# Gate and up projections as 2x2 block products with seven block products each, from the seventh pair of tiles on

## The chip, the cores and the metric

The kernel runs on one core of a Trainium2 chip. The metric is the device time of one execution in microseconds (us). The core has a matrix engine (PE, with its weight loads shown apart as PEld), a vector engine (DVE), a scalar engine (ACT), GpSimd (POOL) and a sync engine (SP), which here issues DMAs. Each engine runs its own instructions in order; they wait for each other through semaphores.

## The reference, cut to what matters

Two transformer blocks run over 512 tokens of width 1024, all in float32. The second block has two feed-forward layers (SwiGLU) of width 2816, and the change is in the first two matrix products of each.

```
D_FF = 2816
def swiglu(x, w_gate, w_up, w_down):
    return (jax.nn.silu(x @ w_gate) * (x @ w_up)) @ w_down

def second_block(x, ...):
    h = x
    f = swiglu(rms_norm(h, g_ffn1_pre[i]), w_ffn1_gate[i], w_ffn1_up[i], w_ffn1_down[i])
    h = h + 0.5 * rms_norm(f, g_ffn1_post[i])
    ...                      # attention
    f = swiglu(rms_norm(h, g_ffn2_pre[i]), w_ffn2_gate[i], w_ffn2_up[i], w_ffn2_down[i])
    h = h + 0.5 * rms_norm(f, g_ffn2_post[i])
    ...
```

## The kernel before

All activations lie transposed, features on the 128 partitions and the 512 tokens along the row. A float32 product is made of three matmuls on the fp32r type (`mm3`, lines 283 to 287): each operand is split into a high part, which ScalarE makes by a copy to fp32r, and a low part, which VectorE makes by subtracting the high part. The three are high by high, low activation by high weight, and high activation by low weight.

The weights are one stream of 218 chunks of 128 rows by 1024 (512 KB). A chunk holds the eight 128x128 tiles, one for each block of 128 input features, that make one tile of 128 output features. SP loads chunk d into slot d % 4 of `RAW`; ScalarE writes its high part to `WH` (`hi_of_weights`, line 622 in the profile, where all of ScalarE's operations are counted), VectorE overwrites `RAW` with its low part (`WL`; `lo_of_weights`, line 1110, and line 1462 in the loop). Counting semaphores order it: `w_hi`, `w_lo` and `mm` count chunks whose high part, low part and matmuls are done; SP loads chunk d when chunk d - 4 has been multiplied.

A feed-forward layer starts with `mlp_up` (chunks D_F1 = 40 to 83, and D_F2 = 140 to 183 of the second layer): 22 pairs of tiles, where a pair is a gate chunk and the up chunk of the same 128 hidden features. The first four chunks run in halves of 256 tokens, since their input is still being normalised; the other 40 are a hardware loop (`Fori(1, 11)`) of ten rounds over four PSUM banks, each chunk 8 x 3 matmuls of 512 columns. `UH` and `UL` hold the input without the factor 1/rms of each token, so VectorE multiplies each product by it (`T[6]`) when it empties the bank: lines 1466 for gate and 1468 for up. ScalarE takes the Silu, VectorE multiplies the two (line 1471), ScalarE writes the high part of the result to `HH` and VectorE the low part to `HL` (line 1473). `f_g`, `f_s`, `f_u`, `f_h`, `f_hh` and `f_hl` count these steps. GpSimd has nothing to do in `mlp_up`; around it, it adds squares for the norms (`sum_y`, `sum_n`, lines 514 and 525).

`mlp_down` follows without a break: 16 chunks at 512 columns and then a tail at 256 columns (`TAIL_H`, `TAIL_L`). `plan_banks` says which event frees each bank; `DOWN_BANK` lists the banks of `mlp_down`.

## Time and profile before

| what | value |
|---|---|
| median of 3 runs | 1502.83 us (1502.73 to 1506.14) |
| the profiled execution, first to last instruction | 1500.5 us |
| PE busy | 1452.3 us (97%) |
| VectorE, ScalarE, GpSimd busy | 828.7, 683.7, 201.9 us |
| chain that ended last | PE 84%, DVE 9%, ACT 3% |
| the 40 full chunks of `mlp_up`, first layer | 217.6 us, from 428.2 to 645.8 us |

The page of the profile gives the totals. Its chain is the path from the last instruction back to what released each one, so it tells which engine sets the end. A matmul's duration in the profile runs over the start of the next one, so the pace of a row of matmuls is read from the distance of their starts. Times "from the start" are from the first instruction of the profiled execution.

### The profile page before, as it was taken

Reading aid. Unit: us, or ns where it says so; the run is one execution under the profiler, and the core shown is the slowest. Engines: PE = TensorE matmul, PEld = TensorE weight load, DVE = VectorE, ACT = ScalarE, POOL = GpSimd, SP = SyncE. Lnnn points to the kernel's source line nnn. Section 1 sums busy time; section 2 is a strip of 40 time slices with the busy share of each in tenths; the row PEclk is TensorE's granted clock in tenths of the full one; section 3 lists DMA queues with packets and bytes.
Section 4 is the critical chain, followed back from the end, with each engine's and each line's share of the span. In section 5 each row is a group of like instructions: output and inputs, shape, how many; then the busy total and the mean of one; then the engine's idle time right before and its main releaser. Section 6 shows DMA issues by size and latency. Waiting matters only on the chain.

```text
span 1500.5 us, 22048 instructions
## 1 busy us (share of the span) xinstructions
PE 1452.3 (97%) x8524; PEld 1226.9 (82%) x8524; DVE 828.7 (55%) x1455; ACT 683.7 (46%) x1302; POOL 201.9 (13%) x319
## 2 busy tenths in 40 slices
PE   7999999899999999999999999989999999999997
PEld 4887876678988888888998777769988888888996
DVE  6678646776645444432275577574754444422474
ACT  4565536676542222221363556676532232321563
POOL 0000000443310000000130222451300000000221
PEclk9999999999999999999999999999999999999999
DMA  9542440004033333333404211503133333332321
GB/s 365 197 167 85 124 157 10 1 2 169 2 99 98 98 98 98 94 95 94 152 3 167 71 57 43 169 16 99 33 109 98 94 92 96 103 105 92 120 85 56
DMA packets 42148, 146.71 MB, mean 98 GB/s; under 512 B 4673, under 2 KB 7121, under 8 KB 41682
## 3 DMA queue, kind: packets, MB, share of 16 engines
q1 hardware_dynamic: 37986, 128.99, 27.2%
q0 software_dynamic: 3072, 15.71, 2.8%
q8 instruction: 54, 0.88, 0.3%
q10 hardware_dynamic: 1008, 0.89, 0.2%
q14 instruction: 28, 0.23, 0.0%
HBM read 141.39 MB, written 4.19 MB: 97 GB/s over the span
## 4 chain that ended last, share of the span: by engine, by line
PE 84%; DVE 9%; ACT 3%; issue 2%; DMA 1%; POOL 0%; DVEq 0%; SPq 0%; ACTq 0%; POOLq 0%
PE B L285 22%; PE B L287 22%; PE B L286 22%; PE CROW_P L285 3%; PE CROW_P L287 3%; PE CROW_P L286 3%; PE B L1789 2%; PE B L2025 1%; DVE AL L1381 1%; DVE WADA L1143 1%; PE CROW_P L1868 1%; ACT T L622 1%; PE CROW_P L1768 1%; ACT AH L622 1%; DVE WL L1110 1%
## 5 line engine op out<-in xcount | busy, mean ns | idle before, releaser
L285 PE MATMUL B<-UH,WH 128*128 128x512 f32 (+1 forms) x1008 | 374.7, 372 | 4.6 <-DVE WL L1110 3.7
L287 PE MATMUL B<-UH,WL 128*128 128x512 f32 (+1 forms) x1008 | 372.3, 369 | 0.0
L286 PE MATMUL B<-UL,WH 128*128 128x512 f32 (+1 forms) x1008 | 372.3, 369 | 0.0
L622 ACT ACTIVATE WH<-RAW 128x1024 fp32r<-128x1024 f32 x174 | 182.6, 1052 | 120.0 <-DMA RAW<-in_stream 111.6
L285 PEld LDWEIGHTS B<-UH,WH 128*128 128x128 f32 x1008 | 190.4, 189 | 38.0 <-issue 5.0
L286 PEld LDWEIGHTS B<-UL,WH 128*128 128x128 f32 x1008 | 190.3, 189 | 32.0
L287 PEld LDWEIGHTS B<-UH,WL 128*128 128x128 f32 x1008 | 190.2, 189 | 32.0
L1110 DVE TENSOR_TENSOR WL<-RAW,WH 128x1024 fp32r<-128x1024 f32 x94 | 116.0, 1240 | 143.8 <-ACT WH L622 143.7
L1462 DVE TENSOR_TENSOR WL<-RAW,WH 128x1024 fp32r<-128x1024 f32 x80 | 98.0, 1226 | 76.7 <-ACT WH L622 73.9
L622 ACT ACTIVATE T<-B 128x256 f32<-128x256 f32 (+5 forms) x186 | 86.5, 465 | 109.9 <-PE B L287 63.3
L622 ACT ACTIVATE T<-T 128x512 f32<-128x512 f32 (+3 forms) x131 | 68.7, 525 | 130.8 <-DVE T L1466 119.2
L514 POOL TENSOR_TENSOR T<-T,T 128x256 f32<-128x256 f32 x60 | 55.0, 918 | 543.0 <-ACT T L622 542.2
L622 ACT ACTIVATE HH<-T 128x512 f32 (+1 forms) x44 | 27.8, 632 | 189.3 <-DVE T L1471 183.3
L285 PE MATMUL B<-HH,WH 128*128 128x512 f32 x192 | 74.7, 389 | 0.0
L286 PE MATMUL B<-HL,WH 128*128 128x512 f32 x192 | 74.7, 389 | 0.0
L287 PE MATMUL B<-HH,WL 128*128 128x512 f32 x192 | 74.7, 389 | 0.0
L285 PE MATMUL B<-UH,KEPT_H 128*128 128x256 f32 (+1 forms) x220 | 66.4, 302 | 1.6 <-DVE KEPT_L L1108 1.6
L1468 DVE TENSOR_TENSOR T<-B,T 128x512 f32<-128x512 f32 x40 | 27.7, 692 | 71.2 <-PE B L287 71.2
L286 PE MATMUL B<-UL,KEPT_H 128*128 128x256 f32 (+1 forms) x220 | 65.9, 299 | 0.0
L287 PE MATMUL B<-UH,KEPT_L 128*128 128x256 f32 (+1 forms) x220 | 65.7, 299 | 0.0
L1381 DVE TENSOR_TENSOR AL<-CROW_P,AH 128x128 fp32r<-128x128 f32 (+3 forms) x96 | 42.5, 483 | 17.3 <-ACT AH L622 17.1
L1473 DVE TENSOR_TENSOR HL<-T,HH 128x512 f32 x40 | 27.7, 693 | 36.6 <-ACT HH L622 36.6
(419 smaller groups left out, 3146.2 us busy)
## 6 DMA issues: line engine op xcount, KB each, us to landing
RAW<-in_stream SPq DMA_DIRECT2D x202, 512.0 KB, 3.7
WADA<-in_w_ada SPq DMA_DIRECT2D x8, 1024.0 KB, 16.7
RAW<-in_stream SPq DMA_DIRECT2D x16, 384.0 KB, 3.5
WADA<-in_w_ada SPq DMA_DIRECT2D x2, 2048.0 KB, 11.5
W<-in_w POOLq DMA_DIRECT2D x2, 2048.0 KB, 12.1
X<-in_x SPq DMA_DIRECT2D x2, 1024.0 KB, 11.0
DECAY<-in_decay POOLq DMA_DIRECT2D x1, 2048.0 KB, 9.6
X<-in_x POOLq DMA_DIRECT2D x2, 1024.0 KB, 8.2
```

The source lines that it names most:

```text
L285: nc.tensor.matmul(out, lh, rh, start=start, stop=False, **kw)
L286: nc.tensor.matmul(out, lh, rl, start=False, stop=False, **kw)
L287: return nc.tensor.matmul(out, ll, rh, start=False, stop=stop, **kw)
L514: E["y_sum"].mark(nc.gpsimd.tensor_tensor(T[7][:, h], T[8][:, h] if k == 1 else T[7][:, h], T[8 + k % 2][:, h], ALU.add))
L622: return nc.scalar.activation(out, in_, func, **kw)
L1110: tt(WL[:, d % SLOTS, :], RAW[:, d % SLOTS, :], WH[:, d % SLOTS, :], ALU.subtract).then_inc(w_lo, 1)
L1143: E["ada_dot"].mark(stt(WADA[:, m, :], WADA[:, m, :], 1.0, (CROW_P if m < 2 * KT else CROW)[:, :], ALU.mult, ALU.mult, accum_out=DOTS[:, m ...
L1381: tag["lo"].mark(tt(AL2[:, u % 4, 0:(i + 1) * P], PT_BANK[s][:, 0:(i + 1) * P], AH2[:, u % 4, 0:(i + 1) * P], ALU.subtract))
L1462: tt(WL[:, nxt, :], RAW[:, nxt, :], WH[:, nxt, :], ALU.subtract).then_inc(w_lo, 1)
L1468: tt(T[4][:, :], B[j][:, :], T[6][:, :], ALU.mult).then_inc(f_u, 1)
L1473: tt(HL[:, i * 2 + j // 2, :], T[5][:, :], HH[:, i * 2 + j // 2, :], ALU.subtract).then_inc(f_hl, 1)
L1789: ins = [mat(outs[s], fixed[s][x], moving[s][y], start=start and x + y == 0, stop=stop and x == 1) for s in range(2)]
```

## The change

Pairs 0 to 4 of each `mlp_up` stay as they are, unrolled. Pair 5 is computed in four blocks of 256 tokens by 512 input features, so that parts of `UH` and `UL` can be overwritten before the pair ends. From pair 6 (`SEVEN = 6`) to 21, gate and up of a pair are one product of a 2x2 block matrix of weights (gate and up, by the two halves of the input features) with a 2x2 block matrix of activations (halves of the features, by halves of the tokens), in seven block products P1 to P7 instead of eight. A block product is 4 x 3 matmuls of 256 columns. Each uses a block or a sum of blocks of weights, and a block or a sum of blocks of activations:

- VectorE normalises the input into `XN` (`normed`); GpSimd makes four sums of its blocks in `TF` (`t_sum`), ScalarE and VectorE their high and low parts (`t_hi`, `t_lo`), seven pieces of 128x1024 in all. `X` gives up its place for some of them; it is written to `x_kept` in device memory and read back when `mlp_up` is done.
- For each pair GpSimd makes four sums of weight blocks of 128x512 (`sevens`, lines 672 to 684 of the changed kernel), and ScalarE and VectorE split seven blocks of 128x512 (`seven_hi`, `seven_lo`) instead of two chunks of 128x1024. The high parts lie in a ring of eight (`W7H`), the low parts overwrite their sources.
- The results are put together from three banks for each pair, six in all (`SEVEN_BANKS`). P6, P7 and P4 go on top of P1 in one bank, P3 on top of P5 in another. ScalarE copies P5, P1 and P1+P6 out of their banks (`snapshot`), and VectorE adds (`gate_half` twice, `up_half`) and multiplies (`hidden_half` twice). A factor 1/rms is no longer needed.
- SP loads the up chunk of a pair ahead of its gate chunk, the up chunk into one of three places, one of which is new (`RAW_T`).

The diff's core, in the order of the file: banks and order of block products, SP's loads, GpSimd's sums of a pair, ScalarE's row of a pair (`highs` are calls of `seven_hi` for the block products of the next pair), and PE before and after.

```diff
-DOWN_BANK = (6, 7, 5, 0, 1, 2, 3, 4)
+DOWN_BANK = (2, 3, 0, 1, 5, 6, 7, 4)
+SEVEN = 6
+PRODUCTS = [(SEVEN, "P5")] + [x for p in range(SEVEN, FT) for x in
+                              [(p, "P1"), (p, "P2"), (p, "P6"), (p, "P3"), (p, "P7")] + [(p + 1, "P5")] * (p + 1 < FT) + [(p, "P4")]]
...
+                at_7 = seven_of(d)
+                if at_7 and at_7[2] == 1:
+                    if at_7[1] == SEVEN:
+                        wait(sp, E["n_rstd"], 2 if at_7[0] == D_F1 else 6)
+                    else:
+                        sp.wait_ge(mm, d - 6 + 1)
...
+                for p in range(SEVEN, FT):
...
+                    pool.wait_ge(*HERE[u])
+                    if p >= SEVEN + 2:
+                        seven_wait(pool, d0, PRODUCT_AT[p - 2, "P5"], E["st"], mm)
...
+                    E["s_sum"].mark(nc.gpsimd.tensor_tensor(s1, a3, a4, ALU.add))
+                    pool.wait_ge(*HERE[g])
+                    if p >= SEVEN + 2:
+                        seven_wait(pool, d0, PRODUCT_AT[p - 2, "P6"], E["st"], mm)
...
+                    wait(pool, E["s_sum"], n + 1)
+                    E["s_sum"].mark(nc.gpsimd.tensor_tensor(s2, s1, a1, ALU.subtract))
+                    E["s_sum"].mark(nc.gpsimd.tensor_tensor(a3, a1, a3, ALU.subtract))
+                    if p >= SEVEN + 2:
+                        seven_wait(pool, d0, PRODUCT_AT[p - 2, "P3"], E["st"], mm)
+                    wait(pool, E["s_sum"], n + 2)
+                    E["s_sum"].mark(nc.gpsimd.tensor_tensor(s4, a2, s2, ALU.subtract))
...
+                    highs(0)
...
+                    highs(1)
+                    if p > SEVEN:
+                        hidden_hi(p - 1)
+                    snapshot(p, "P1")
+                    highs(2)
+                    snapshot(p, "U2")
+                    highs(3)
...
+                    highs(4)
+                    silu(p)
+                    highs(5)
+                    if p + 1 < FT:
+                        snapshot(p + 1, "P5")
+                    highs(6)
...
-                with pe.Fori(1, 11) as i:
-                    for j in range(4):
-                        pe.wait_ge(w_lo, i * 4 + (d0 + j + 1))
-                        pe.wait_ge((f_g, f_u)[j % 2], i * 2 + (n0 + j // 2 - 1))
-                        for k in range(KT):
-                            ins = mm3(B[j][:, :], wtile(WH, j, k), wtile(WL, j, k), UH[:, k, :], UL[:, k, :], k == 0, k == KT - 1)
-                        ins.then_inc(mm, 1)
...
+                for q, (p, name) in enumerate(PRODUCTS):
...
+                    seven_wait(pe, d0, q, E["s_lo"], w_lo)
+                    if name in ("P1", "P2", "P5") and p < SEVEN + 2:
+                        pe.wait_ge(f_h, n0 + p - 1)
...
+                    elif name == "P4":
+                        pe.wait_ge(f_u, n0 + p + 1)
+                    else:
+                        wait(pe, E["s_cp"], copy_count(d0, p, {"P6": "P1", "P7": "U2", "P3": "P5"}[name]))
...
+                    for k in range(4):
+                        ks = slice(k * P, (k + 1) * P)
+                        ins = mm3(out[:, 0:HALF], hi[:, ks], lo[:, ks], moving[name][0][:, k, :], moving[name][1][:, k, :],
+                                  name in ("P1", "P2", "P5") and k == 0, k == 3, skip_group_check=True)
```

VectorE in the loop of `mlp_up` before, one pair (two chunks); `T_181` is the factor 1/rms, `T_175` the gate, `T_179` the up product, `T_180` the hidden values:

```order
L1462 TENSOR_TENSOR WL<-RAW,WH 128x1024 [waits w_hi]
L1466 TENSOR_TENSOR T_175<-B,T_181 128x512 [waits mm]
L1462 TENSOR_TENSOR WL<-RAW,WH 128x1024 [waits w_hi]
L1468 TENSOR_TENSOR T_179<-B,T_181 128x512 [waits mm]
L1471 TENSOR_TENSOR T_180<-T_179,T_177 128x512 [waits f_s,f_u]
L1473 TENSOR_TENSOR HL<-T_180,HH 128x512
```

VectorE in the changed kernel, first layer, from a pair's `gate_half` (L1741, twice) over `up_half` (L1749) and `hidden_half` (L1756) to the low part of P5 two pairs on, the low part of the next pair's P4 and the second `hidden_half` (L1759); L1734 is `seven_lo`:

```order
L1741 TENSOR_TENSOR T0_192<-CROW_P,T7_199 128x256 [waits x_sq,mm]
L1734 TENSOR_TENSOR SUM_L2_170<-T2_194,W7H_165 128x512 [waits gain_cols,q_hi]
L1734 TENSOR_TENSOR SUM_L11_172<-T11_203,W7H_165 128x512 [waits gain_cols,q_hi]
L1741 TENSOR_TENSOR T0_192<-B4,T7_199 128x256 [waits x_sq,ret_s]
L1734 TENSOR_TENSOR WL_57<-RAW_55,W7H_165 128x512 [waits gain_cols,q_hi]
L1749 TENSOR_TENSOR T1_193<-CROW_P,T1_193 128x256 [waits x_sq,ret_s]
L1756 TENSOR_TENSOR T5_197<-T1_193,T0_192 128x256 [waits f_s,f_u]
L1734 TENSOR_TENSOR SUM_L6_169<-T6_198,W7H_165 128x512 [waits gain_cols,q_hi]
L1734 TENSOR_TENSOR WL_57<-RAW_55,W7H_165 128x512 [waits gain_cols,w_hi]
L1759 TENSOR_TENSOR T5_197<-CROW_P,T0_192 128x256 [waits mm]
```

One pair had six VectorE instructions; it now has thirteen, and the second half of the hidden values stands behind the low parts of two weight blocks.

GpSimd had no instruction between the last `sum_n` of the layer's start and the first `sum_y` of its end; there it now has, for each pair (this is pair 8 of the first layer), in the changed kernel:

```order
L672 TENSOR_TENSOR T10_202<-RAW_55 128x512 [waits ret_s,raw_here3]
L679 TENSOR_TENSOR T2_194<-T10_202,RAW_55 128x512 [waits gain_cols,ret_s,raw_here0]
L680 TENSOR_TENSOR RAW_55<-RAW_55 128x512
L684 TENSOR_TENSOR T11_203<-RAW_55,T2_194 128x512 [waits gain_cols,ret_s]
L672 TENSOR_TENSOR T6_198<-RAW_T_166 128x512 [waits ret_s,c_here]
```

The first four are one pair's sums and the fifth opens the next pair. `raw_here3` and `raw_here0` are the arrivals of the up and the gate chunk, `ret_s` counts block products that PE has finished two pairs back, `gain_cols` GpSimd's own sums.

## Rows read from the trace of the kernel before

**Rows 1.** The page: busy time of each engine, granted clock, and the chain's engines.

```profile
PE 1452.3 (97%) x8524; PEld 1226.9 (82%) x8524; DVE 828.7 (55%) x1455; ACT 683.7 (46%) x1302; POOL 201.9 (13%) x319
...
PEclk9999999999999999999999999999999999999999
...
PE 84%; DVE 9%; ACT 3%; issue 2%; DMA 1%; POOL 0%; DVEq 0%; SPq 0%; ACTq 0%; POOLq 0%
```

**Rows 2.** Busy time by stretch (us, PE, PEld, DVE, ACT, POOL, clock); PE's groups there.

```profile
433.60:651.20 217.60, 217.60 (x961) 180.18 (x961) 105.68 (x123) 66.31 (x84) 0.00 (x0) 1.00 0.33 97
...
L285 PE MATMUL B<-UH,WH 128*128 128x512 f32 x312 | 121.4, 389 | 0.0
```

**Rows 3.** Timeline (start, duration, what): a chunk's first matmul, and the next chunk's.

```profile
504.36 0.39 PE L285 MATMUL B<-UH,WH 128*128 128x512 f32 x1
...
509.80 0.39 PE L285 MATMUL B<-UH,WH 128*128 128x512 f32 x1
```

**Rows 4.** Timeline: matmuls of 256 columns, the first and the 34th in a row.

```profile
732.84 0.28 PE L285 MATMUL CROW_P<-HH,TAIL_H 128*128 128x256 f32 x1
...
736.79 0.28 PE L285 MATMUL CROW_P<-HH,TAIL_H 128*128 128x256 f32 x1
```

**Rows 5.** Timeline of the other engines around the end of a chunk at 504.36.

```profile
499.85 0.63 ACT L622 ACTIVATE T<-T 128x512 f32<-128x512 f32 x1 [3.04 <-DVE T L1466]
...
500.38 1.04 ACT L622 ACTIVATE WH<-RAW 128x1024 fp32r<-128x1024 f32 x1
...
504.55 5.77 SPq L435 DMA_DIRECT2D RAW<-in_stream  x2
504.56 0.69 DVE L1468 TENSOR_TENSOR T<-B,T 128x512 f32<-128x512 f32 x1 [1.87 <-PE B L287]
...
505.29 0.69 DVE L1471 TENSOR_TENSOR T<-T,T 128x512 f32<-128x512 f32 x1
...
506.10 0.63 ACT L622 ACTIVATE HH<-T 128x512 f32 x1 [4.67 <-DVE T L1471]
```

**Rows 6.** Groups by shape: copies from PSUM on ScalarE, a 256-column operation on VectorE.

```profile
L622 ACT ACTIVATE T<-B 128x256 f32<-128x256 f32 x94 | 35.9, 382 | 83.7 <-PE B L287 53.7 <-PE B L1659 18.0 <-PE B L1649 8.7
...
L1117 DVE TENSOR_TENSOR T<-YE,T 128x256 f32<-128x256 f32 x16 | 6.6, 420 | 0.0
```

**Rows 7.** DMA issues from 500 to 640 us: count, size, median us to landing.

```profile
RAW<-in_stream SPq DMA_DIRECT2D x25, 512.0 KB, 3.6
```

**Rows 8.** Timeline of VectorE and GpSimd where both work, 256 columns.

```profile
762.32 0.74 POOL L525 TENSOR_TENSOR T<-T,T 128x256 f32<-128x256 f32 x1 [2.18 <-ACT T L622]
762.37 0.97 DVE L1117 TENSOR_TENSOR T<-Y_U,T 128x256 f32<-128x256 f32 x1
763.02 0.93 POOL L514 TENSOR_TENSOR T<-T,T 128x256 f32<-128x256 f32 x1
...
763.26 0.96 DVE L1121 SCALAR_TENSOR_TENSOR X<-T,SC,X 128x256 f32<-128x256 f32 x1
763.90 0.92 POOL L525 TENSOR_TENSOR T<-T,T 128x256 f32<-128x256 f32 x1
764.15 0.96 DVE L1128 SCALAR_TENSOR_TENSOR UL<-X,VECS,UH 128x256 fp32r<-128x256 f32 x1
```

**Rows 9.** The same with 384 and 512 columns, and two in a row.

```profile
915.23 1.29 POOL L569 TENSOR_TENSOR SQA<-SQA 128x512 f32<-128x512 f32 x1
...
915.85 1.08 DVE L1525 TENSOR_TENSOR ALS<-T,AHS 128x384 fp32r<-128x384 f32 x1 [1.27 <-ACT AHS L622]
916.86 0.68 DVE L1520 TENSOR_TENSOR SP0L<-T,SP0H 128x512 fp32r<-128x512 f32 x1
917.46 0.68 DVE L1563 TENSOR_TENSOR KBL<-T,KBH 128x512 fp32r<-128x512 f32 x1
```

**Rows 10.** Groups by shape: low parts on VectorE, 1024 columns, and 384 alone.

```profile
L1462 DVE TENSOR_TENSOR WL<-RAW,WH 128x1024 fp32r<-128x1024 f32 x40 | 49.0, 1226 | 38.3 <-ACT WH L622 37.0
...
L1520 DVE TENSOR_TENSOR SPL<-T,SPH 128x384 fp32r<-128x384 f32 x8 | 4.4, 552 | 0.0
```

**Rows 11.** Timeline: GpSimd against a VectorE operation that reads PSUM and SBUF.

```profile
983.15 1.36 POOL L489 TENSOR_SCALAR T<-T,RECS,CONST 128x128 f32<-128x128 f32 x2 [1.52 <-DVE RECS L1387]
983.68 0.41 DVE L1373 CUSTOM_DVE_ANT_0 T<-B,BIAS 128x256 f32<-128x256 f32 x1
```

**Rows 12.** The page's DMA issues: reading X back from device memory.

```profile
X<-in_x POOLq DMA_DIRECT2D x2, 1024.0 KB, 8.2
```

More of the change, by code:

```diff
@@ new lines, in mlp_up @@
+                for c in range(12):
+                    if c < 2:
+                        hi_of_weights(d0 + c + 4)
+                    elif 4 <= c < 10:
+                        hi_of_weights(d0 + c + 2)
+                    if c in (8, 9, 10):
+                        t_hi(c - 8)
+                    if c == 10:
+                        seven_hi(0)
+                        seven_hi(1)
+                        t_hi(3)
+                        seven_hi(2)
+                        t_hi(4)
+                        seven_hi(3)
+                        t_hi(5)
+                    if c % 2 == 0:
+                        silu(c // 2)
+                    elif c < 11:
+                        hidden_hi(c // 2)
@@ L923, in mlp_down @@
+                hidden_hi(FT - 1)
             def mlp_down(d0, t, scale):
```

381 lines of the change are left out of this document (319 added, 62 removed).

## The prediction

> **What bounds the kernel now.** I read the page first: PE is busy 97% of the span and makes 84% of the chain that ended last, at a granted clock of nine tenths or more in every slice (2.4 GHz) [rows 1]. Then the stretch of the full chunks of the first `mlp_up`: PE never idles in its 217.6 us, while VectorE is busy 105.7, ScalarE 66.3 and GpSimd 0.00 us [rows 2]. So only PE's own work sets the time there, and the other three have room. A matmul's duration overlaps the next, so its price is the distance of starts: a chunk of 24 at 512 columns takes 509.80 - 504.36 = 5.44 us, 226.7 ns each [rows 3]; 33 at 256 columns take 736.79 - 732.84 = 3.95 us, 119.7 ns each, 120 below, across two changes of bank [rows 4]. Half the columns cost 53% of the time, not 50%.
>
> **PE's own share.** A pair before: 48 matmuls, 2 x 5.44 = 10.88 us. A pair by seven block products: 7 x 12 = 84 matmuls of 120 ns, 1.44 us a block product, 10.08 us. Gain 0.80 us a pair; 16 pairs in each of two layers give 25.6 us. The second layer's loop has the same instructions, so I price it as the first. Pair 5 is now 96 matmuls of 256 columns: 11.52 against 10.88 us, +0.64 in each layer, +1.3 us. If nothing waits: 24.3 us less.
>
> **Work on the others, per pair.** ScalarE: seven splits of 512 and the Silu and hidden copy, each 0.53 us start to start [rows 5], and three copies of 256 from PSUM at 0.38 [rows 6]: 9 x 0.53 + 1.1 = 5.9 us, of 10.08. VectorE: seven low parts and one `HL`, 0.60 us start to start [rows 9], and five operations of 256 columns at 0.42 [rows 6]: 6.9 us. GpSimd: four sums of 1.29 us [rows 9]: 5.2 us. Each fits alone. Two things decide whether they fit together.
>
> First, **GpSimd and VectorE exclude each other** on operations with two SBUF inputs. In rows 8 three VectorE operations of 256 columns, 0.42 us alone, take 0.96 to 0.97 us each while GpSimd adds, and the two engines take strict turns of 0.88 us. In rows 9 an operation that takes 0.55 alone [rows 10] starts at 915.85 beside a GpSimd addition begun at 915.23 and takes 1.08: it was held until 915.85 + 1.08 - 0.55 = 916.38, 1.15 us after GpSimd's start. One that reads PSUM and SBUF isn't held (0.41 us) [rows 11]. From 0.74 at 256 and 1.29 at 512 columns, GpSimd streams 1.10 us of the 1.29, and the start-up of a second one can lie under VectorE's turn. `seven_lo`, `HL` and the first `hidden_half` have two SBUF inputs; `gate_half`, `up_half` and the last `hidden_half` have one.
>
> Second, **every engine is in order, with the next step behind something else**. Block products in one bank leave a gap of one between them: P1 is copied out while P2 runs, then P6 may start; P6's sum while P3 runs, then P7; P7's sum (`up_half`) while P5 of the next pair runs, then P4. The hand-over takes 0.20 us from PE's end to the next engine's start [rows 5], 0.38 for the copy and some 0.1 back: 0.7 of 1.44 us, so 0.75 is spare. But ScalarE copies P1 of a pair out only after the hidden copy of the pair before (`hidden_hi`), and that waits for VectorE's last `hidden_half`, which stands behind the low parts of P5 and P4, which share their port with GpSimd.
>
> **The sum round the cycle.** I follow it from the end of P2 of pair p. SP then issues the gate chunk of pair p+2: 0.19 us [rows 5], 3.6 to land [rows 7]. GpSimd adds s2 (1.15), and VectorE, waiting with the low part of P7, takes its turn (0.60); GpSimd a3 (1.10), VectorE `hidden_half` (0.35); GpSimd s4 (1.10), VectorE the low parts of P5 and P4 (1.20) and the other `hidden_half` (0.42). Hand-over and `hidden_hi` on ScalarE 0.63 (0.10 and 0.53), copy of P1 0.38, PE goes on 0.1. Total 0.19 + 3.6 + 1.15 + 0.60 + 1.10 + 0.35 + 1.10 + 1.20 + 0.42 + 0.63 + 0.38 + 0.1 = 10.82 us, and then P6 of pair p+1 may start. From the start of a P6 to the end of the next P2 PE has seven block products, 10.08 us. The two stretches together are two periods: (10.82 + 10.08) / 2 = 10.45 us a pair, with 0.37 us of waiting before each P6.
>
> How sure is the 10.82? With each turn 0.1 shorter, and GpSimd's start-up wholly hidden, it is some 10.3 (period 10.2); with full durations (0.69 for a low part, 1.29 for a sum) in place of the turns it is 11.5 (period 10.8). I take the turns, since rows 8 and 9 show the two engines in just this situation. A pair then gains 10.88 - 10.45 = 0.43 us.
>
> **The first pair of the new kind** can't be a steady one. VectorE has to get through four low parts of 128x1024 around the end of pair 5, and the last of them stands ahead of the emptying of chunk 11, since `t_lo(6)` waits for a piece of `UH` that is free only when pair 5 ends. From that end: `t_hi(6)` and `t_lo(6)` 0.2 + 1.04 + 1.23 = 2.5 us [rows 5, 10], emptying 0.7, `hidden` 0.7, `hidden_hi` on ScalarE 0.6, three splits 1.6, copy of P1 0.4, hand-overs some 0.3: 6.8 us, while P6 would start 3 x 1.44 = 4.3 us after pair 5. Waiting 2.5 us, and about 0.7 more at P4, where three low parts stand ahead of `up_half`: 3.2 us a layer. Bounds: 0 and 5.
>
> **What costs nothing, and under what.** The other pieces of `XN`, `TF` and their splits (VectorE 8 x 0.7 + 3 x 1.23 = 9.3 us [rows 10], ScalarE 3 x 1.04, GpSimd 4 sums of 1024 columns, about 2.4 each) lie in pairs 1 to 4, 43 us, where VectorE is idle half the time [rows 2]. The 2 MB of X out and back in each layer: 8.2 us a megabyte-sized transfer [rows 12], started when `mlp_up` ends and needed only after `mlp_down`'s tail, some 110 us on. The first chunks of `mlp_down` are split in pair 21, where no next pair is split. The unrolled loop: elsewhere PE already runs unrolled at 120 ns [rows 4].
>
> **Total.** Thirty steady pairs gain 30 x 0.43 = 12.9. The two first pairs gain 2 x 0.80 and lose 2 x 3.2: +4.8. Pair 5: +1.3. Together 6.8 us less. Of the profiled execution's own 1500.5 us that leaves 1493.7; the median of the runs lies 2.3 us above it, for what lies around the span, so I forecast 1502.8 - 6.8 = **1496.0 us**.
>
> **Rivals.** (A) The forecast, period 10.2 to 10.65: thirty pairs gain 20.4 to 6.9 us, total 1488.5 to 1502. (B) PE hardly waits: the turns interlock more kindly, or the gate chunk lands in under 3 us, and the cycle closes below 10.08. For it: VectorE has 3 us a pair to spare and splits run a whole pair ahead, so only the hidden chain is tight. Against it: the turns of rows 8 were strict. It gives 1478.5 with the first pairs free, 1485 with them as above. (C) The other side: the port is full. VectorE's two-input operations are 8 x 0.69 + 0.42 = 5.9 us a pair and GpSimd's 4 x 1.29 = 5.2; if they exclude each other for their whole durations, a pair can't take less than 11.1 us. Thirty pairs then lose 6.6, and with the 6.1 of the first pairs and pair 5 it is 1502.8 + 12.7 = 1515.5 us. It decides from a period of 10.68 on (30 x 0.20 = 6.1). For it: `up_half` then comes behind a turn of GpSimd at each pair and P4 waits too. Against it: rows 8 have 0.74 + 0.42 = 1.16 us of work in 0.88. (D) The clock: stops at each product let the granted clock fall from 2.4 to 1.2 GHz. The page shows no such slice, though PE idles 3% of the span [rows 1]; I leave it inside (C).
>
> The Trainium skill, "SBUF — State Buffer", section "Who interferes with whom", states the rule behind rows 8 and (C): a VectorE instruction with two SBUF inputs contends with a GpSimd instruction that reads SBUF, and the loser waits until the first has finished. The trace agrees on who is held and who isn't [rows 8, 9, 11]. Its section on the two sides of SBUF has the lock held for the whole instruction, which would be (C), 1515.5 us; here 0.88 us for a turn says that part of a duration isn't covered by the lock, which gives (A).
>
> **Numbers.** (A) 0.48, (B) 0.27, (C) 0.25, whose nearer half reaches from 1502 to 1508. About 0.3% (4.5 us) is what a measurement of this kernel can tell from no change. Faster by more, below 1498.3: all of (B) and 0.31 of (A), 0.58. Within it: 0.17 of (A) and 0.05 of (C), 0.22. Slower by more, above 1507.3: 0.20. The range runs from 1480 to 1513: it leaves out the kindest part of (B) and the worst of (C), about one in ten each.
>
> **What would show it.** Starts of matmuls 120 ns apart within a block product: PE's share is right; at 130 it would be 30 x 0.84 us worse. PE's idle time ended mostly by ScalarE's copy ahead of P6: the cycle is right; by VectorE ahead of P4, (C) is. VectorE's `seven_lo` with a mean well over 0.69 us: turns with GpSimd. The distance of two P1 of the same bank, halved, is the period: 10.45 for (A), 10.1 for (B), 11 for (C). The first P6 of a layer 2 to 3 us late. If PE waits for low parts themselves, or for a DMA, my cycle is the wrong one.

## The result and the profile after

| kernel | median | runs | ratio to before, 95% interval |
|---|---|---|---|
| before | 1504.49 us | 4 (1502.73 to 1506.55) | |
| changed | 1527.92 us | 4 (1524.49 to 1535.79) | 1.017 (1.0151 to 1.019) |

The changed kernel is 1.7% slower. The forecast was 1496.0 us with a range to 1513: wrong in sign and outside the range. The profiled execution of the changed kernel is the longest of the four, so its rows overstate the loss by some microseconds. One execution of a later kernel (vector_by_need, experiment 9) took 1982.19 us at a mean granted clock of 0.652, where its other four lie between 1485.96 and 1491.04 us at 0.989 to 0.993; its ratio leaves that execution out.

The page of the changed kernel, the lines that answer to [rows 1]:

```profile
PE 1451.6 (95%) x9772; PEld 1279.8 (83%) x9772; DVE 1028.2 (67%) x1709; ACT 795.4 (52%) x1572; POOL 430.2 (28%) x463
...
PEclk8999999999999999999999999999998999999999
...
PE 70%; DVE 16%; issue 5%; ACT 5%; DMA 1%; POOL 1%; DVEq 0%; SPq 0%; ACTq 0%; POOLq 0%
```

PE's share of the chain fell from 84 to 70%, and VectorE's rose from 9 to 16%. VectorE is busy 199.5 us more than before. Of these, 254 instructions explain only a part: the rest is time in which it was held, as the groups of `seven_lo` by shape show (count, busy us, mean ns of one). Alone such a low part takes 0.68 [rows 9].

```profile
L1734 DVE TENSOR_TENSOR SUM_L<-T,W7H 128x512 fp32r<-128x512 f32 x96 | 115.5, 1221 | 4.9 <-ACT W7H L779 3.2
...
L1734 DVE TENSOR_TENSOR WL<-RAW,W7H 128x512 fp32r<-128x512 f32 x104 | 95.6, 920 | 10.4 <-ACT W7H L779 6.3
```

Busy time by stretch, columns as in [rows 2]. First the 40 full chunks of each layer (217.6 us before); then what lies around the first new pair; then twelve later pairs in each layer, from P1 of pair 8 to P1 of pair 20:

```profile
431.97:663.99 232.02, 215.22 (x1586) 205.32 (x1585) 208.50 (x252) 121.65 (x218) 110.93 (x68) 0.97 0.30 99
1107.06:1339.92 232.86, 214.59 (x1587) 205.25 (x1585) 207.09 (x252) 120.25 (x217) 111.84 (x68) 0.97 0.31 100
...
482.00:505.00 23.00, 14.58 (x98) 14.22 (x97) 20.29 (x21) 9.50 (x19) 12.71 (x8) 0.80 0.21 67
...
515.97:644.09 128.12, 124.47 (x1011) 121.79 (x1010) 123.72 (x157) 75.26 (x144) 73.26 (x49) 1.00 0.32 100
1188.69:1319.97 131.28, 125.73 (x1010) 123.25 (x1009) 122.73 (x157) 75.14 (x144) 74.22 (x49) 0.99 0.32 97
```

The layers are 14.4 and 15.3 us longer, 29.7 of the 33.5 us by which the two profiled executions differ. In the fourth row twelve pairs take 128.12 / 12 = 10.68 us each, and VectorE is busy 123.72 of the 128.12 us, 97%, where [rows 2] had it half idle. PE's waits in the first layer (what it waited for: us in total, times, longest):

```profile
PE B L306 <- DVE T L1749: 6.8, 2, 6.0
PE B L306 <- ACT T L779: 3.9, 3, 2.4
PE B L306 <- DVE WL L1359: 3.8, 2, 2.8
PE CROW_P L306 <- DVE T L1749: 0.6, 1, 0.6
```

L1749 is `up_half` on VectorE, ahead of P4; L779 is ScalarE's copy, ahead of P6; L1359 is the low part of a plain chunk. Short waits, such as the small ones ahead of each P6, aren't in this list, so I also took the layer apart by the starts of PE's block products. If nothing waited, six plain chunks, pair 5 and 112 block products would take 6 x 5.44 + 11.52 + 112 x 1.44 = 205.4 us, 12.2 less than before in each layer. What the stretches took beyond that, in us:

| excess over no waits | layer 1 | layer 2 |
|---|---|---|
| pairs 2 to 5 | 5.8 | 2.5 |
| P5 of pair 6 to P1 of pair 7: 23.08 and 24.17 instead of 11.52 | 11.6 | 12.7 |
| 14 periods: 10.68 and 10.90 instead of 10.08 | 8.4 | 11.4 |
| P4 of the last pair, and what follows it | 0.9 | 0.9 |

**The first new pair.** GpSimd's timeline from the moment the places for the sums of pair 7 are free:

```profile
485.97 1.27 POOL L672 TENSOR_TENSOR T<-RAW 128x512 f32<-128x512 f32 x1 [10.43 <-DVE T L1706]
487.41 1.50 POOL L679 TENSOR_TENSOR T<-T,RAW 128x512 f32<-128x512 f32 x1 [0.17 <-POOL T L672]
488.87 1.72 POOL L680 TENSOR_TENSOR RAW<-RAW 128x512 f32<-128x512 f32 x1
...
492.24 1.75 POOL L672 TENSOR_TENSOR T<-RAW 128x512 f32<-128x512 f32 x1
...
497.32 1.70 POOL L684 TENSOR_TENSOR T<-RAW,T 128x512 f32<-128x512 f32 x1
```

The four sums of pair 7 and the four of pair 8 run back to back, eight in 13 us. VectorE and PE beside them:

```profile
489.38 1.76 DVE L1734 TENSOR_TENSOR LOW_T<-RAW_T,W7H 128x512 fp32r<-128x512 f32 x1
491.07 1.77 DVE L1734 TENSOR_TENSOR SUM_L<-T,W7H 128x512 fp32r<-128x512 f32 x1
...
494.46 3.44 DVE L1734 TENSOR_TENSOR WL<-RAW,W7H 128x512 fp32r<-128x512 f32 x2
...
501.73 0.42 DVE L1749 TENSOR_TENSOR T<-B,T 128x256 f32<-128x256 f32 x1
```

```profile
488.83 0.36 PE L306 MATMUL B<-T2H,W7H 128*128 128x256 f32 x1 [2.44 <-ACT T L779]
...
502.29 0.55 PE L306 MATMUL B<-T4H,W7H 128*128 128x256 f32 x1 [5.99 <-DVE T L1749]
```

A low part takes 1.7 us instead of 0.7, as each waits for a sum; `up_half` stands behind them, and P4 waits 5.99 us for it. So the 11.6 us of this pair are 2.4 of waiting at P6, 6.0 at P4, and the rest, some 3 us, mostly the clock behind the two waits.

**Ahead of it.** The sums of the input blocks (1024 columns) hold VectorE in the same way, and the chunk computed in blocks needs its twin too:

```profile
456.16 3.45 DVE L1359 TENSOR_TENSOR WL<-RAW,WH 128x1024 fp32r<-128x1024 f32 x1 [1.65 <-ACT WH L779]
...
468.91 0.58 PE L306 MATMUL B<-UH,WH 128*128 128x256 f32 x1 [2.81 <-DVE WL L1359]
```

**The clock.** Around the first new pair the granted clock is 0.80 in the window shown. In the block products behind the long waits a matmul starts 0.14 to 0.23 us after the last on the mean instead of 0.12; a part or all of each was at 1.2 GHz (granted clock 0.50 from 489.50 to 492.40 and from 503 to 506 us). The steps above 120 ns inside the block products sum to 4.4 us in the first layer and 5.5 in the second. They are contained in the table.

### The profile page after: what moved, and what is told of

The parts are those of the page before. It is cut to its first block, busy times and chain, and to the rows that moved or that the text cites. A ratio compares the mean times of both kernels' runs of the same rounds, so it can differ in the third digit from the quotient of the medians.

```text
span 1534.0 us, 25604 instructions
## 1 busy us (share of the span) xinstructions
PE 1451.6 (95%) x9772; PEld 1279.8 (83%) x9772; DVE 1028.2 (67%) x1709; ACT 795.4 (52%) x1572; POOL 430.2 (28%) x463
## 3 DMA queue, kind: packets, MB, share of 16 engines
q8 instruction: 79, 1.29, 0.4%
## 4 chain that ended last, share of the span: by engine, by line
PE 70%; DVE 16%; issue 5%; ACT 5%; DMA 1%; POOL 1%; DVEq 0%; SPq 0%; ACTq 0%; POOLq 0%
PE B L306 16%; PE B L307 15%; PE B L308 15%; PE CROW_P L306 5%; PE CROW_P L308 5%; PE CROW_P L307 5%; PE B L2133 2%; DVE WL L1359 2%; ACT T L779 2%; PE B L2408 1%; PE CROW_P L2212 1%; DVE WADA L1392 1%; DVE AL L1630 1%; DVE SUM_L L1734 1%; DVE XN L1716 1%
## 5 line engine op out<-in xcount | busy, mean ns | idle before, releaser
L1359 DVE TENSOR_TENSOR WL<-RAW,WH 128x1024 fp32r<-128x1024 f32 x110 | 140.0, 1278 | 152.4 <-ACT WH L779 152.1
L308 PE MATMUL B<-UH,WL 128*128 128x256 f32 (+1 forms) x656 | 216.2, 330 | 0.0
L306 PE MATMUL B<-UH,WH 128*128 128x512 f32 (+1 forms) x528 | 182.3, 345 | 10.6 <-DVE WL L1359 9.7
L779 ACT ACTIVATE T<-B 128x256 f32<-128x256 f32 (+5 forms) x250 | 110.6, 442 | 152.6 <-PE B L308 103.1
L779 ACT ACTIVATE WH<-RAW 128x1024 fp32r<-128x1024 f32 x110 | 115.8, 1058 | 123.8 <-DMA RAW<-in_stream 113.1
L307 PE MATMUL B<-UL,WH 128*128 128x512 f32 (+1 forms) x528 | 179.7, 340 | 0.0
L306 PEld LDWEIGHTS B<-UH,WH 128*128 128x128 f32 x528 | 101.0, 191 | 24.2 <-DVE WL L1359 7.3
L1734 DVE TENSOR_TENSOR SUM_L<-T,W7H 128x512 fp32r<-128x512 f32 x96 | 115.5, 1221 | 4.9 <-ACT W7H L779 3.2
L307 PEld LDWEIGHTS B<-UL,WH 128*128 128x128 f32 x528 | 101.1, 191 | 10.6
L306 PE MATMUL B<-UH,W7H 128*128 128x256 f32 x384 | 109.8, 286 | 0.0
L307 PE MATMUL B<-UL,W7H 128*128 128x256 f32 x384 | 109.7, 286 | 0.0
L1734 DVE TENSOR_TENSOR WL<-RAW,W7H 128x512 fp32r<-128x512 f32 x104 | 95.6, 920 | 10.4 <-ACT W7H L779 6.3
L779 ACT ACTIVATE T<-T 128x512 f32<-128x512 f32 (+3 forms) x131 | 68.6, 525 | 50.5 <-DVE T L1697 23.1
L779 ACT ACTIVATE W7H<-RAW 128x512 fp32r<-128x512 f32 x104 | 65.2, 627 | 33.6 <-PE B L308 23.1
L306 PEld LDWEIGHTS B<-UH,W7H 128*128 128x128 f32 x384 | 75.0, 195 | 0.0
## 6 DMA issues: line engine op xcount, KB each, us to landing
WADA<-in_w_ada SPq DMA_DIRECT2D x2, 2048.0 KB, 10.5
```

The lines of the kernel that those rows point to most:

```text
L306: nc.tensor.matmul(out, lh, rh, start=start, stop=False, **kw)
L307: nc.tensor.matmul(out, lh, rl, start=False, stop=False, **kw)
L308: return nc.tensor.matmul(out, ll, rh, start=False, stop=stop, **kw)
L779: return nc.scalar.activation(out, in_, func, **kw)
L1359: tt(WL[:, d % SLOTS, :], RAW[:, d % SLOTS, :], WH[:, d % SLOTS, :], ALU.subtract).then_inc(w_lo, 1)
L1734: seven_mark(q, tt(lo, src, seven_high(q), ALU.subtract), E["s_lo"], w_lo)
```

## Experiments

All ratios are to the kernel before, run on the same chip in the same rounds. A period is the distance from P1 to the P1 of the next pair.

**1. one_column: GpSimd's sums made nearly free**

```diff
-                    E["s_sum"].mark(nc.gpsimd.tensor_tensor(s1, a3, a4, ALU.add))
+                    E["s_sum"].mark(nc.gpsimd.tensor_tensor(s1[:, 0:1], a3[:, 0:1], a4[:, 0:1], ALU.add))
...
-                return T[SUM_AT[name][p % 2]][:, :], SUM_L[name, p % 2][:, :]
+                return raw_tile(d0 + 2 * p + 1)[:, 512:1024], SUM_L[name, p % 2][:, :]
```

(the other three sums alike)

> Left out: GpSimd's four sums of a pair add one column of 512, and the three block products that use them take a half of the up chunk instead; the number of instructions, their order and all waits stay. Theory T (the sums and the turns they force on VectorE are what costs): the first new pair falls from 23.1 and 24.2 us to at most 14 us in each layer (-18 to -22 us for both), the later periods from 10.68 and 10.90 us to 10.08 to 10.20 (-16 to -20 us for both layers), so 1486 to 1496 us beside 1527.9. Rival O (the order in which ScalarE and VectorE are told to work holds TensorE up whatever GpSimd does): the first pair stays above 19 us and the periods at or above 10.4 us, so 1515 to 1528 us. In between: first pair much shorter, periods still 10.35 to 10.45 by the two hand-overs of the hidden tile, about 1500 us.

1496.11 us, ratio 0.9954 (0.9941 to 0.9966). The first pair takes 15.51 and 15.52 us, more than the 14 that the theory allowed; every later period takes 10.08. That the time is the forecast's 1496.0 us is chance: this kernel leaves out what the forecast had priced. Twelve pairs, from P1 of pair 8:

```profile
502.99:623.95 120.96, 120.96 (x1010) 120.96 (x1009) 86.65 (x157) 75.51 (x144) 14.25 (x48) 1.00 0.34 106
```

The same instructions in the same order, and PE never waits there; VectorE is busy 86.65 / 12 = 7.22 us a pair instead of 10.31. So the order and the number of instructions don't hold PE up by themselves; the duration of the sums does. It also shows what is left when they cost nothing: 4.0 us at the first pair in each layer, and a gain of 0.5% at the most for this order of work.

**2. copy_first: ScalarE's order at P6**

```diff
+                    snapshot(p, "P1")
                     if p > SEVEN:
                         hidden_hi(p - 1)
-                    snapshot(p, "P1")
```

> ScalarE copies the P1 block of a pair out of its bank before it makes the high part of the hidden tile of the pair before. Theory (the 0.3 to 0.7 us that TensorE waits ahead of each P6 come from VectorE's half of the hidden tile and ScalarE's high part of it standing ahead of that copy): the wait ahead of P6 goes, the periods after the first pair fall from a mean of 10.79 to 10.1 to 10.4 us, 28 periods give 11 to 19 us back, 1509 to 1517 us beside 1527.9; the first pair stays at 23 us. Rival (the cycle of transfers, sums and low parts is as long as before and the wait only moves to another product, P2, P3 or P7): periods at or above 10.6 us, 1525 to 1529 us.

1527.26 us, ratio 1.0159 (1.0142 to 1.0177): nothing gained. The waits ahead of P6 are gone (4.6 us in the later pairs of the first layer before, 0.0 now), but those ahead of P4 rose in their place, from 2.5 to 6.3 us in the later pairs of the first layer and from 3.4 to 4.5 in the second (0.8 of each is the last pair's P4); periods are 10.73 in the first layer and 10.42 in the second. PE's waits for `up_half` in the first layer:

```profile
PE B L306 <- DVE T L1749: 11.1, 6, 7.5
```

The rival is right in the time and in the first layer's periods; it had not named P4, and the second layer's periods fell below its 10.6 us without a gain in the median. ScalarE's copy was the last link that showed, and behind it VectorE was late anyway. Twelve pairs of the first layer have VectorE busy 124.24 of 128.49 us:

```profile
514.08:642.57 128.49, 124.26 (x1011) 122.87 (x1010) 124.24 (x157) 76.03 (x144) 73.82 (x49) 0.99 0.32 99
```

**3. first_pair: the first pair in order of need**

The edit of copy_first, and, among other moves in the first pair:

```diff
-                    if p >= SEVEN + 2:
+                    if p == SEVEN + 2:
+                        seven_wait(pool, d0, PRODUCT_AT[p - 1, "P1"], E["st"], mm)
+                    elif p > SEVEN + 2:
                         seven_wait(pool, d0, PRODUCT_AT[p - 2, "P5"], E["st"], mm)
...
+                seven_lo(5)
+                gate_half(SEVEN, 0)
+                seven_lo(6)
+                seven_lo(7)
+                gate_half(SEVEN, 1)
+                seven_lo(8)
+                up_half(SEVEN)
```

> Beside the edit of copy_first: in the first new pair of each layer ScalarE and VectorE take their steps in the order in which TensorE needs them, the gate and up sums of that pair ahead of low parts that are needed later, and GpSimd's sums for the pair after next wait until P1 of the second new pair is done. Theory (the 11.6 and 12.6 us that the first new pair loses are the order: the up half stands behind six low parts that each take a turn with GpSimd): the first pair falls from 23.1 and 24.2 us to 12 to 15 us, 17 to 22 us less than copy_first. Rival (there is simply more work ahead of the first pair than the engines can do, so what is put back is missing one pair later): first and second pair together stay at or above 31 us, and the time is within 6 us of copy_first.

1526.97 us, ratio 1.0163 (1.0132 to 1.0193). The first pair fell to 13.79 and 14.85 us, as the theory said, and the second rose from 10.98 and 10.80 to 19.95 in both layers. Together they are 33.7 and 34.8 us, against 34.1 and 35.0. The rival is right again: now the sums of pairs 8 and 9, which the edit starts together, run back to back, eight in 12.9 us, and P4 of the second pair waits instead of the first's.

```profile
494.44 1.83 POOL L674 TENSOR_TENSOR T<-RAW 128x512 f32<-128x512 f32 x1 [5.22 <-PE CROW_P L308]
...
505.67 1.71 POOL L686 TENSOR_TENSOR T<-RAW,T 128x512 f32<-128x512 f32 x1
```

```profile
509.94 0.55 PE L306 MATMUL CROW_P<-T4H,W7H 128*128 128x256 f32 x1 [8.45 <-DVE T L1776]
```

**4. setup: the order ahead of the new kind**

```diff
-                    if 4 <= c < 10:
-                        lo_of_weights(d0 + c + 2)
+                    if c == 8:
+                        lo_of_weights(d0 + c + 3)
...
+                    if 3 <= c < 8:
+                        lo_of_weights(d0 + c + 3)
                     if c in (1, 3, 4, 5):
                         for k in range(2):
                             normed({1: 0, 3: 2, 4: 4, 5: 6}[c] + k)
```

(and the same chunk earlier on ScalarE)

> Only the pairs ahead of the new kind: VectorE makes the low part of a chunk ahead of the normed tiles that only the sums need, and high and low part of the twelfth chunk are made one chunk earlier on both engines, since the eleventh and twelfth are now computed in blocks and need both at the start. Theory (the 5.8 and 2.5 us lost ahead of the new kind are these two orders): the waits ahead of the seventh and the eleventh chunk go, 5 to 8 us less than 1527.9, 1520 to 1523 us. Rival (GpSimd's sums of 1024 columns hold VectorE, 3.45 us for a low part that alone takes 1.22): at least 4 of the 8 us stay, or come back at the first new pair, 1524 to 1528 us.

1528.61 us, ratio 1.0167 (1.0151 to 1.0184). From the first full chunk to P5 of pair 6 it took 44.4 us in the first layer (49.95 in the changed kernel, 44.2 without waits), but the first pair became longer, 24.42 and 25.62 us. Nothing was gained: what PE gets ahead here it waits for at P6, since the sums of pair 7 can't start before pair 5's hidden tile is out of their places.

**5. fourth_sum_twice: one sum more on GpSimd**

```diff
+                    if p >= SEVEN + 2:
+                        E["s_sum"].mark(nc.gpsimd.tensor_tensor(s4, a2, s2, ALU.subtract))
...
+                    wait(pool, E["s_sum"], n + 4)
                     E["s_sum"].mark(nc.gpsimd.tensor_tensor(s4, a2, s2, ALU.subtract))
```

(in the two pairs before that, the added sum has one column)

> GpSimd makes the fourth sum of each pair from the third new pair on twice, the second time when the first is done (1.29 us alone, about 1.72 us in turns with VectorE). Theory T (the pairs' period is the cycle that runs through GpSimd's sums and VectorE's low parts beside them): each period is longer by 0.5 to 0.9 us (the cycle spans two periods), 28 periods give 14 to 25 us, 1542 to 1553 us beside 1527.9. Rival (order and clock, not the sums, hold the period at 10.7 us; GpSimd is idle 35 to 40% of it): no more than 3 us longer, 1528 to 1531 us.

1560.24 us, ratio 1.0379 (1.0362 to 1.0396): 32.3 us more than the changed kernel, above both expectations. GpSimd is busy 93.83 / 12 = 7.8 us in a pair and has a third of its time free, and still:

```profile
513.18:654.28 141.10, 126.28 (x1011) 123.33 (x1010) 135.31 (x157) 74.83 (x144) 93.83 (x61) 0.99 0.30 90
```

A pair takes 141.10 / 12 = 11.76 us, 1.08 more, and VectorE is busy 135.31 / 12 = 11.28, 0.97 more. A cycle over two periods would have passed on half of the added turn (0.5 to 0.9 us). In these twelve pairs the period rose by what VectorE's busy time rose, and more; by the medians it is 32.3 / 28 = 1.15 us a period. The profiled executions alone tell less in the second layer, where all 14 periods rose by 0.88 us, from 10.90 to 11.78, since the changed kernel's has a late transfer there. And the cycle isn't absent: six times in the first layer a period of 12.4 to 13.7 us stands next to one of 10.1 to 10.5. What part of the loss it makes stays open.

**6. vector_sums: the sums on VectorE**

```diff
-                    E["s_sum"].mark(nc.gpsimd.tensor_tensor(s1, a3, a4, ALU.add))
+                    if part == 0:
+                        dve.wait_ge(*HERE[u])
+                        E["s_sum"].mark(tt(s1, a3, a4, ALU.add))
...
+                    if p + 2 < FT:
+                        w_sum(p + 2, 0)
+                        w_sum(p + 2, 1)
```

(`w_sum` makes one of the four sums; the other two stand at the start of the next pair)

> GpSimd's four sums of a pair go to VectorE, in its own order of work, one or two pairs later than GpSimd made them (GpSimd keeps only the sums of the input columns ahead of the new kind). Theory T (a sum on GpSimd costs VectorE about 1.0 us of turns, on VectorE itself 0.6 us, so the move frees VectorE although it gets more to do): VectorE has 7 x 0.60 + 4 x 0.60 + 5 x 0.36 + 0.65 = 9.1 us of work a pair of 10.08, the periods after the first pair fall to 10.08 to 10.3 us (-11 to -20 us for both layers), the first pair from 23.1 and 24.2 to 14 to 18 us (-12 to -18 us), 1490 to 1505 us beside 1527.9. Rival (VectorE is the full engine and gets 2.4 us a pair more): periods at or above 10.7 us, 1528 us or more.

1509.83 us, ratio 1.0044 (1.0027 to 1.0061), 18 us less than the changed kernel. VectorE got 128 instructions more and is busy 1002.2 us in all, 26 less than the 1028.2 above. The time is above the theory's 1490 to 1505 us, because the first two pairs gave little: 18.11 and 18.56 us for the first and 14.4 and 14.5 for the second, together 32.5 and 33.1 against 34.1 and 35.0. From the third pair on the periods are 10.08.

```profile
511.74:632.70 120.96, 120.96 (x1011) 120.96 (x1009) 114.26 (x205) 74.02 (x145) 0.00 (x0) 1.00 0.34 106
```

VectorE's load is 114.26 / 12 = 9.52 us a pair (9.1 was expected). So four sums cost VectorE (9.52 - 7.22) / 4 = 0.58 us each when it makes them, and (10.31 - 7.22) / 4 = 0.77 us each when GpSimd does, not the 1.0 of the expectation. The move does a second thing: a sum is finished in one short step, where a sum on GpSimd takes up to 1.75 us in turns. This run doesn't tell the two apart.

**7. vector_all: with the orders of 2 and 4**

The edits of vector_sums, copy_first and setup together, of which again:

```diff
+                    snapshot(p, "P1")
                     if p > SEVEN:
                         hidden_hi(p - 1)
-                    snapshot(p, "P1")
...
+                    if 3 <= c < 8:
+                        lo_of_weights(d0 + c + 3)
```

> vector_sums with the edits of copy_first and setup on top. Theory: with the turns gone, what these two edits give is kept instead of lost again at the next product: 3 to 8 us less than vector_sums, 1485 to 1500 us. Rival (they move waits only, as on top of the changed kernel): within 2 us of vector_sums.

1504.52 us, ratio 1.0014 (1.0004 to 1.0024), 5.3 us less than vector_sums, though above the expected 1485 to 1500; the two edits that gave nothing on the changed kernel give something here. First pair 19.7 and 20.6 us, second 12.4 and 12.2.

**8. vector_first_pair: and the first pair in order of need**

```diff
-                    evict(c)
+                    if c == 11:
+                        t_lo(5)
+                        seven_lo(3)
+                        evict(10)
+                        evict(11)
+                        t_lo(6)
+                        seven_lo(4)
+                        hidden(11)
```

(and ScalarE's copies of P5 and P1 ahead of its splits for pair 7)

> vector_all, and in the first new pair ScalarE and VectorE take their steps in the order of TensorE's need: ScalarE copies P5 and P1 out of their banks ahead of the high parts of the next pair, VectorE evicts the last two plain chunks ahead of the last low part of the input and makes the sums of the second new pair and the up half ahead of what is needed later. Theory (with the turns gone the first pair's loss is order and can be taken away, unlike in first_pair): P5 of the first pair to P1 of the second falls from 19.7 and 20.6 us to 12.5 to 15 us, the second pair from 12.45 and 12.19 to 10.1 to 11 us, together 12 to 20 us less than vector_all: 1485 to 1493 us beside 1502.6 of before. Rival (the work that stands ahead of the first pair is too much for VectorE in whatever order; what one product gains the next loses): the two pairs together stay within 3 us of the 32.2 and 32.8 us of vector_all, 1501 to 1505 us.

1497.63 us, ratio 0.9968 (0.9953 to 0.9982), 6.9 us less than vector_all. The first pair takes 12.90 us in both layers, inside the theory's bounds; the second takes 15.81, since all low parts still had to get a whole pair ahead there. Half the expected gain.

**9. vector_by_need, and 10. gpsimd_by_need: the order of need in all pairs, with either engine's sums**

```diff
+                for p in range(SEVEN + 1, FT):
+                    q = PRODUCT_AT[p, "P1"]
...
+                    seven_lo(q + 2)
+                    hidden_half(p - 1, 0)
...
+                    seven_lo(q + 3)
...
+                    seven_lo(q + 4)
+                    hidden_lo(p - 1)
+                    gate_half(p, 0)
...
+                    gate_half(p, 1)
...
+                    up_half(p)
```

VectorE's low parts are made one or two block products ahead instead of a pair ahead. vector_by_need has `w_sum` between them, gpsimd_by_need has GpSimd's sums of the changed kernel.

> vector_first_pair, and all later pairs too are in the order of TensorE's need: VectorE makes each low part 2 to 3 us before its product instead of a whole pair before, so that the second new pair has nothing to catch up. Theory: VectorE has 9.1 to 9.7 us of work in a pair of 10.08, the second new pair falls from 15.81 to 10.1 to 11.5 us, the rest stays at 10.08: 8 to 11 us less than vector_first_pair, 1486 to 1490 us, 13 to 17 us below before (1502.9). Rival (with the low parts only just ahead of TensorE any lateness reaches it): the periods rise to 10.3 to 10.6 us, 28 of them take 6 to 14 us, and the time is 1492 to 1504 us.

> The same order of work as in vector_by_need, but the four sums of a pair back on GpSimd, as in the changed kernel; so this tells the order from the turns. Theory T (it is the turns): the order alone gives back little, since VectorE has 9 us of work of its own and some 4 us of turns in a pair of 10.08: periods at or above 10.5 us and the first two pairs together at or above 31 us, 1518 to 1530 us beside 1527.9 of the changed kernel. Rival O (it was the order all along, the move to VectorE only came with it): periods 10.1 to 10.3 us and the first two pairs together below 26 us, 1490 to 1500 us.

vector_by_need: 1488.42 us, ratio 0.9904 (0.9887 to 0.9921), 1.0% faster than before and 2.6% faster than the changed kernel. First pair 12.90, second 10.99, all others 10.08 us. gpsimd_by_need: 1511.50 us, ratio 1.0049 (1.003 to 1.0068); first 15.4 and 16.4, second 15.0 and 14.0, then 10.33 and 10.37 us on the mean. The same twelve pairs of both, the second row with GpSimd's sums:

```profile
499.08:620.04 120.96, 120.96 (x1011) 120.96 (x1009) 111.23 (x206) 73.01 (x146) 0.00 (x0) 1.00 0.34 106
```

```profile
509.02:632.94 123.92, 123.55 (x1010) 121.52 (x1009) 114.78 (x158) 72.63 (x145) 72.76 (x48) 1.00 0.33 103
```

The low parts on VectorE in vector_by_need, and PE's waits in its first layer:

```profile
L1716 DVE TENSOR_TENSOR WL<-RAW,W7H 128x512 fp32r<-128x512 f32 x104 | 71.4, 687 | 3.3
L1716 DVE TENSOR_TENSOR SUM_L<-T,W7H 128x512 fp32r<-128x512 f32 x96 | 65.7, 684 | 0.0
```

```profile
PE B L306 <- DVE WL L1341: 1.3, 1, 1.3
PE B L306 <- ACT T L755: 0.7, 1, 0.7
PE CROW_P L306 <- DVE WL L1716: 0.7, 1, 0.7
PE CROW_P L306 <- DVE T L1731: 0.6, 1, 0.6
```

Neither theory had it whole. The order alone (with those of copy_first and setup, which it contains) gives 16.4 us, 1527.9 to 1511.5, where I had expected under 10; the move to VectorE, with the old order, 18.1; both together 39.5. That is 5.0 more than the sum of the two, which the intervals (about 3 us for each kernel) don't tell from the sum. VectorE's load depends on the order too: with GpSimd's sums it is 114.78 / 12 = 9.57 us a pair here, so a sum costs it (9.57 - 7.22) / 4 = 0.59 us, not 0.77; with its own sums in this order it is 9.27, or 0.51 a sum. But with GpSimd's sums the first two pairs still take 30.4 us, against 23.9. And the later periods stay 0.25 and 0.29 us over 10.08 with VectorE only 93% busy: PE starts each P2 but a few 0.10 to 0.28 us late, which its list of waits doesn't show. VectorE's load doesn't account for that. What in the turns does, perhaps that a low part comes late because it waits for a sum, wasn't tested.

**11. one_more, and 12. three_more: how much more VectorE can carry**

```diff
                         E["s_sum"].mark(tt(s4, a2, s2, ALU.subtract))
+                        for again in range(1):
+                            wait(dve, E["s_sum"], n + 4 + again)
+                            E["s_sum"].mark(tt(s4, a2, s2, ALU.subtract))
```

(three_more has `range(3)`)

> vector_by_need with the fourth sum of each pair made twice on VectorE, one after the other. VectorE was busy 111.2 us in twelve pairs there, 9.27 us a pair; one more sum of 0.69 us with its wait on the first makes 10.0 us of 10.08. Theory F (the pairs' period is the larger of TensorE's 10.08 us and VectorE's whole load, its own work and the time it is held): periods stay at 10.08 to 10.2 us, 0 to 4 us more than 1488.4. Rival (what matters is how far low parts run ahead of TensorE, so that every 0.7 us added shows): periods of 10.5 to 10.8 us, 12 to 20 us more.

> The same with the fourth sum made four times: 9.27 + 3 x 0.71 = 11.4 us of work on VectorE a pair. Theory F: periods of 11.3 to 11.6 us, 1.2 to 1.5 us over 10.08, in 30 pairs 36 to 46 us more than vector_by_need, 1524 to 1535 us; VectorE busy 97% or more of the steady stretch. Rival (the chain of hand-overs sets the period): every added sum shows with its whole 0.7 us from the first on, so this is 3 times what one_more adds; by F it is far more than 3 times.

one_more: 1490.45 us, ratio 0.9926 (0.991 to 0.9943), 2.0 us more than vector_by_need. three_more: 1538.41 us, ratio 1.0246 (1.0229 to 1.0263), 50.0 us more, above the expected 36 to 46. Of the 48.2 us between the two profiled executions 43.7 lie in the pairs of the new kind, 7.3 of them in the two second pairs, which took 14.65 us; another 4.6 us lie ahead of them, where P5 of pair 6 now starts 2.3 us late in each layer. Twelve pairs of each:

```profile
498.41:619.37 120.96, 120.96 (x1011) 120.96 (x1009) 118.28 (x217) 73.03 (x144) 0.00 (x0) 1.00 0.34 106
```

```profile
504.52:640.96 136.44, 124.01 (x1011) 121.58 (x1009) 133.42 (x241) 73.50 (x144) 0.00 (x0) 1.00 0.30 94
```

With VectorE 98% busy PE still never waits (118.28 of 120.96 us, periods 10.08 from the third pair on); with two sums more the period is 11.37 us, as worked out from 9.27 + 3 x 0.71. A fixed 0.7 us a sum would have given 20 us for one_more. So with the sums on VectorE the period is the larger of TensorE's 10.08 us and VectorE's load. With GpSimd's sums it came out above both: 10.68 with a load of 10.31, 11.76 with 11.28, and 10.33 with 9.57.

## Why the prediction was wrong

**PE's own share** was right: 120.0 ns from matmul to matmul in undisturbed block products, 1.44 us a block product, 10.08 us a pair where nothing waits, 12.2 us less a layer. Outside the two stretches nothing was lost to the change: in the profiled execution the first stretch starts 3.8 us later, but 1.5 us of these are there by 204 us and 3.6 by 209 us from the start, in work that is the same in both kernels. The forecast put the profiled execution at 1493.7 us and it took 1534.0. Of these 40.3 us the first new pairs make 17.9 (24.3 instead of 6.4), the later pairs 10.5 (21.6 instead of 11.1), the pairs ahead of the new kind 8.3, and the 3.8 just named are the rest.

**"Each fits alone. Two things decide whether they fit together."** This step failed. I counted VectorE at 6.9 us a pair (one_column shows 7.22) and GpSimd at 5.2, and let the turns lengthen only those steps that lie on one chain of hand-overs. The sum that was missing is VectorE's own: 6.9 us and four holds. With the 1.10 us that I gave GpSimd's stream in each turn it would have been 6.9 + 4 x 1.10 = 11.3 us at the worst, and it measured 10.31 (0.77 a hold), over 10.08 either way. So VectorE had no time left in a pair of 10.08 us, where I had written that it had 3 us to spare. That a full VectorE sets the period is shown by one_more and three_more, where its load is its own work alone; the 0.4 to 0.7 us by which the later pairs' 10.68 and 10.90 us exceed it isn't split up by any run.

**"The sum round the cycle."** The period of most single pairs was 10.41 to 10.6 us, close to the forecast of 10.45, and most P6 came late (at 550.74 the start is 0.42 us after the last one instead of 0.12). The waits ahead of P6 average 0.33 us over the 14 later pairs of the first layer and 0.39 in the second, against 0.37 forecast. That looked like a confirmation, and the runs don't bear it out: copy_first took these waits away and gained nothing, and fourth_sum_twice made the chain longer by one turn and cost 1.15 us a period, where half a turn was due. That the number of the chain fitted was luck in good part: P4 waited too, 2.5 and 3.4 us in the later pairs of the two layers, 0.8 of each at the last one, and the sum had nothing for it. On top of the typical pair came single long ones. One in the second layer took 13.78 us: its gate chunk took 5.1 us to land instead of 3.5, and the sums started late.

```profile
1196.95 1.53 POOL L679 TENSOR_TENSOR T<-T,RAW 128x512 f32<-128x512 f32 x1 [2.78 <-DMA RAW<-in_stream]
```

P4 then waited 1.97 us, and the clock fell for the next two block products. VectorE, 97% busy, had nothing to make up such a delay with. I had no term for it.

**"The first pair of the new kind", 3.2 us.** Measured 11.6 and 12.7, and this is the largest error, 17.9 us in the two layers. I followed ScalarE and VectorE through the hand-over as if GpSimd weren't there. Without its sums it is 4.0 us (one_column), inside my bounds of 0 to 5, so what I did count was sized well: P6 of pair 6 starts 2.6 and 3.7 us late, where 2.5 was forecast. The term that failed is P4, 0.7 us forecast and 6.0 measured, and the clock behind the waits, priced at nothing. What I left out are the eight sums that become possible all at once when pair 5's hidden tile is gone: 13 us in which VectorE gets one low part per 1.7 us. In first_pair a new order of this pair only moved the loss by a pair; the order of need in all pairs, with GpSimd's sums still there, took 4 us of it (30.4 against 34.1 and 35.0 for the first two pairs).

**"What costs nothing", pairs 1 to 4.** 5.8 and 2.5 us. Half of VectorE's time was idle there, but the input's sums hold it up to 2.2 us at a time, and pair 5 in blocks asks for two chunks at its start. On the changed kernel this cost nothing in the end, since the first pair waited for GpSimd anyway (setup); it shows once that wait is gone (vector_all).

**The clock**, which I left inside (C), cost 4.4 and 5.5 us in the profiled execution, mostly behind the waits of the first new pair.

**The rivals.** (C), the full port, named the right engine pair, with 1515.5 us as its time and 0.25 as its chance. Its sign, VectorE ahead of P4, came with (A)'s: in the two layers PE waits 18.9 us ahead of P4 and 16.4 ahead of P6. Its mechanism was too narrow: it asked whether two engines' durations exclude each other (5.9 + 5.2), not whether VectorE with its holds has the time. The Trainium skill, "SBUF — State Buffer", section "Who interferes with whom", has the loser wait until the first instruction has finished. The rows here say less: a low part of 0.69 and a sum of 1.29 take 1.67 to 1.69 us in turns from start to start, not 1.98. But what follows from the wait, that the one engine's work is time taken from the other, was the part to use, and vector_sums agrees: taking the work off GpSimd made VectorE's busy time shorter.

## What to carry to other kernels

For each engine, add to its own work the time for which other engines hold it, and compare that sum with the period that the bounding engine would have. Where the sum was above it, it didn't fit (10.31 against 10.08 here); one below it still lost where the engines take turns (9.57, and the period was 10.33). Where a second engine only helps by taking turns with the first, try its work on the first. And price the change-over into a new steady state as a sum of all the work that becomes possible or due at once, on every engine, before ordering it by need: reordering one copy or one pair on the changed kernel only moved these waits, and the order of need in all pairs gave 16 us with GpSimd's sums and 21 with VectorE's.

## What the hardware showed that I had not expected

- A sum of 512 columns costs VectorE 0.58 us when VectorE makes it and 0.77 when GpSimd does; in the order of need it is 0.51 and 0.59. An addition that takes VectorE 0.68 us takes GpSimd 1.29 alone.
- Turns of 512 columns are as strict as those of 256 in [rows 8]: 1.67 to 1.69 us from one to the next for a pair of operations that take 0.69 and 1.29 alone, for 13 us on end.
- The clock falls behind a single wait: at P4 of pair 6, after 5.99 us without a matmul, its twelve matmuls start 0.23 us apart on the mean, at a granted clock of 0.50. After the 1.97 us wait at 1211.35 the twelve matmuls of P4 still came at 0.12, and those of the next block product at 0.21 (granted clock 0.99 and 0.50). In vector_by_need, with no wait over 1.3 us in the layer, the largest mean step in a block product is 129 ns.
